# Moving the z, g and half of the output projection of an SSD/retention mixer in among its sample-state updates, and taking q times a retention state before the state is updated, in plain fp32

## The reference, cut to what matters

```python
z, xbc, dt_raw, rq, rk, rv, rg = _split(h @ w_in, AB_SIZES)   # widths 2048, 3072, 32, 1024, 1024, 2048, 2048
...                                                           # causal conv and silu on xbc
y, ssm_h = ssd_scan(xs, dt, a, bm, cm, ssm_h)                 # h = exp(dt a) h + dt x B^T ; y = h C
y = (y + xs * d_skip[:, None]).reshape(...) * jax.nn.silu(z)
y = group_rms(y, SSD_GROUPS) * ssd_norm
r, ret_s = retention_scan(q, k, v, ret_s)                     # S = gamma S + k v^T ; o = q S
r = jax.nn.silu(rg) * group_rms(r.reshape(bsz, l, RET_V), RET_HEADS)
return jnp.concatenate([y, r], axis=-1) @ w_out, conv_buf, ssm_h, ret_s
```

## Time and profile before

| what | us |
|---|---|
| median of 3 runs (2172.78 to 2183.26) | 2179.12 |
| the profiled execution's own time | 2174.99 |
| its span, first to last instruction | 2173.2 |
| TensorE (PE) busy | 1906.6, 88% |
| VectorE (DVE) busy | 1375.7, 63% |
| ScalarE (ACT) busy | 896.0, 41% |
| GpSimd (POOL) busy | 202.1, 9% |
| mean granted TensorE clock | 0.922 |

### The profile page before, as it was taken

How to read it: one execution, slowest core, us unless ns; L and a number is a source line. 1 busy time by engine, 2 the same in 40 slices (tenths; PEclk the granted TensorE clock), 3 DMA queues, 4 the chain that set the end, 5 groups by cost and what they waited for, 6 DMA issues and landing times. The chain is left out here.

```text
span 2173.2 us, 35020 instructions
## 1 busy us (share of the span) xinstructions
PE 1906.6 (88%) x13769; PEld 1744.7 (80%) x13769; DVE 1375.7 (63%) x2352; ACT 896.0 (41%) x1143; POOL 202.1 (9%) x292
## 2 busy tenths in 40 slices
PE   6999886996688768998899999999968698899996
PEld 5999786985355467987779999999956597679996
DVE  4665595698767565448567656665652567557654
ACT  4434344346655445332434334433422532434331
POOL 0001101101111000111110011001001021110011
PEclk9999998899799888998999999999985898999998
DMA  6656852336778424666526656656606266526652
GB/s 179 181 163 188 156 168 65 113 117 189 247 261 298 148 79 114 176 233 232 203 90 182 184 160 191 186 157 195 191 29 163 78 217 229 206 86 174 185 160 82
DMA packets 462782, 361.49 MB, mean 166 GB/s; under 512 B 12297, under 2 KB 435493, under 8 KB 462629
## 3 DMA queue, kind: packets, MB, share of 16 engines
q1 hardware_dynamic: 409056, 254.35, 39.9%
q0 software_dynamic: 20192, 71.95, 10.8%
q10 hardware_dynamic: 33424, 33.70, 4.6%
HBM read 321.49 MB, written 38.66 MB: 166 GB/s over the span
## 5 line engine op out<-in xcount | busy, mean ns | idle before, releaser
L211 DVE TENSOR_TENSOR wlo<-raw,whi 128x2048 fp32r<-128x2048 f32 (+2 forms) x262 | 558.9, 2134 | 268.4 <-ACT whi L205 267.7
L252 PE MATMUL psum<-xnh,whi 128*128 128x264 f32 x2328 | 676.9, 291 | 10.1 <-DVE cols L885 9.8
L253 PE MATMUL psum<-xnl,whi 128*128 128x264 f32 x2328 | 668.7, 287 | 0.0
L254 PE MATMUL psum<-xnh,wlo 128*128 128x264 f32 x2328 | 667.5, 287 | 0.0
L205 ACT ACTIVATE whi<-raw 128x2048 fp32r<-128x2048 f32 (+2 forms) x262 | 463.3, 1770 | 190.7 <-DMA raw<-in_w_ffn_out 76.8
L252 PEld LDWEIGHTS psum<-xnh,whi 128*128 128x128 f32 x2328 | 449.0, 193 | 15.7 <-DVE cols L885 8.6
L253 PEld LDWEIGHTS psum<-xnl,whi 128*128 128x128 f32 x2328 | 448.8, 193 | 1.2
L254 PEld LDWEIGHTS psum<-xnh,wlo 128*128 128x128 f32 x2328 | 445.9, 192 | 0.0
L252 PE MATMUL psum<-Hh,whi 128*128 128x264 f32 x704 | 200.5, 285 | 0.0
L254 PE MATMUL psum<-Hh,wlo 128*128 128x264 f32 x704 | 200.0, 284 | 0.0
L253 PE MATMUL psum<-Hl,whi 128*128 128x264 f32 x704 | 199.1, 283 | 0.0
(11 more groups left out here) (479 smaller groups left out, 3425.3 us busy)
## 6 DMA issues: line engine op xcount, KB each, us to landing
raw<-in_w_ffn_in SPq DMA_DIRECT2D x176, 512.0 KB, 4.9
raw<-in_w_in_ab SPq DMA_DIRECT2D x88, 512.0 KB, 4.4
raw<-in_w_ffn_out SPq DMA_DIRECT2D x64, 384.0 KB, 4.0
raw<-in_w_ffn_out SPq DMA_DIRECT2D x64, 320.0 KB, 3.3
sb<-in_state_ret POOLq DMA_DIRECT2D x32, 512.0 KB, 5.6
out<-sb ACTq DMA_DIRECT2D x32, 512.0 KB, 4.8
raw<-in_w_out_ab SPq DMA_DIRECT2D x32, 512.0 KB, 4.5
kc<-in_cache_mem_k POOLq DMA_DIRECT2D x32, 512.0 KB, 5.9
```

Source lines behind the costliest of these rows:

```text
L211: nc.vector.tensor_tensor(wlo[:, c % SLOTS, 0:m], raw[:, c % SLOTS, 0:m], whi[:, c % SLOTS, 0:m].bitcast(F32), ALU.subtract).then_inc(lo_d ...
L252: e.matmul(out, a, hi[:, kk, 0:S.cols], start=first, stop=False)
L253: e.matmul(out, a, lo[:, kk, 0:S.cols], start=False, stop=False)
L254: m = e.matmul(out, b, hi[:, kk, 0:S.cols], start=False, stop=final)
```

## The change

`Linear` gets a third table, `mid`, whose stages PE runs in the middle of a chunk and DVE and ACT run right behind the split of chunk r+2. Then:

- `SSDSample` is cut in 16 stages of one half state, `RetPrompt` in single scores, values and states; all of them stand in `mid` and `hooks` of the z projection, together with the transposes. `SSDSample` takes one PSUM bank for each half state and spreads B and C rows with one matmul (`spread40`: high parts in rows 0 to 7, remainders in rows 32 to 39 of one tile).
- `RetSample` becomes `RetItem`, one state. PE takes the state as it was loaded as the stationary operand, with one column of q (eight products of 128x128 by 128x1 in fp32), then ACT decays it and DVE adds k v one item later. Since q S_new = gamma (q S_old) + (q.k) v, `RetOut` adds the second term for four tiles of a head. The rounding `sh`, the remainder `sl`, `rrow` and their transposes are gone. States are spread over the g projection and the first half of the output projection, one in each half chunk (four in chunk 0 of g).
- The multiplication by silu(z) and silu(g) for the prompt is put off by one chunk (`gated_late`); the samples' part is kept aside (`zs`, `gs`).
- `Stat` and `Apply` of y and r, group by group, go in the tables of g; the samples' r has its own small `Stat` and `RetSplit`.
- The output projection is two projections of eight chunks: y first (added to x by DVE), then r.
- `mixer_c` uses `Rows40` and `spread40` in place of `SplitRows` and `spread`.

```diff
@@ Linear.pe, in the loop over t and k
+                            if 2 * (t * S.kt + k + 1) == S.tiles * S.kt:
+                                S.hook("pe", e, i, r, S.mid)
@@ Linear.both
                     S.split_later(split, e, i, r + LEAD)
+                    S.hook(which, e, i, r, S.mid)
                     if S.early:
...
+        def spread40(e, out, b, rows):
+            return e.matmul(out, sel[0:40, b:b + 1].to_broadcast([40, P]), rows, start=True, stop=True)
...
+            class SSDSample(Stage):
...
+                def pe(S, e):
+                    u = S.u
+                    if u == 0:
+                        e.wait_ge(rows_lo, bc_rows_ready)
+                    if u >= 2:
+                        e.wait_ge(hy_done, 8 * (u - 1))
+                    c = 256 * (u % 2)
+                    spread40(e, psum[:, 4 + u % 2, :].rearrange("p (q n) -> p q n", q=2), u // 2, BC[:, :, c:c + 256]).then_inc(bcb_done, 1)
...
+            class RetStart(Stage):
+                def pe(S, e):
+                    e.wait_ge(qk_made, 1)
+                    e.wait_ge(hy_done, 16 * NS)
+                    for d in range(2):
+                        m = e.matmul(psum[:, 5, QC:QC + 32], ones[:, :], qks[:, d:8:2, :], start=d == 0, stop=d == 1)
...
+            class RetItem(Stage):
+                def pool(S, e):
+                    j = S.i + SB
+                    if j < N_RET:
+                        e.wait_ge(s_out[buf(j)], 16 * (j // SB))
+                        load_s(e, j)
+                def pe(S, e):
+                    i = S.i
+                    b, h = item(i)
+                    v_row(e, i)
...
+                    e.wait_ge(s_in[buf(i)], 16 * (i // SB + 1))
+                    for t in range(4):
+                        c = OC + (4 * h + t) * NS + b
+                        for d in range(2):
+                            m = e.matmul(psum[:, 5, c:c + 1], sb[:, buf(i), d, t * P:(t + 1) * P], qs[:, 2 * h + d, b:b + 1], start=d == 0, stop=d == 1)
+                    m.then_inc(s_used, 1)
...
+                def act(S, e):
+                    i = S.i
                     if i >= 2:
+                        S.keep(e, i - 2)
+                    e.wait_ge(s_used, i + 1)
+                    v = sb[:, buf(i), :, :]
+                    nc.scalar.activation(v, v, ACT.Copy, scale=gam[item(i)[1]]).then_inc(sdec, 1)
...
+                def dve(S, e):
+                    if S.i >= 1:
+                        S.update(e, S.i - 1)
...
+            def gated_late(dst, stash, q0, final, ready=None):
...
+                def dve(e, l, par, use):
+                    e.tensor_tensor((sg, ht)[par][:, :, :], psum[:, 2 * par:2 * par + 2, 0:T], rstd_two, ALU.mult).then_inc(gate_scaled, 1)
+                    if l >= 1:
+                        mul(e, l - 1, 1 - par)
...
+            points = [[bc_rows, SampleStart()] + v_turn, v_turn2, k_turn,
+                      [RetScores(0, vt_ready)],
+                      [RetValues(0), RetState(0, after_scores(0))],
+                      [RetValues(1), RetScores(1, after_state(0))],
...
+            for u in range(15):
+                points[u + 1].append(SSDSample(u))
+            points[15].extend([SSDSample(15), z_last, SSDOut(), RetStart()])
+            Linear(W, 8, KD, 2, by_cols(W, 0), (xnh, xnl), act=az, dve=dz, mid={c: points[2 * c] for c in range(8)},
+                   hooks={c: points[2 * c + 1] for c in range(8)})
...
+            ret_at = [[RetItem(0), RetItem(1)], [RetItem(2), RetItem(3)]] + [[RetItem(s + 2)] for s in range(2, 30)] + [[], [], []]
...
+            ahead = {0: r_stat(0), 1: y_stat(0)}
+            hook = {0: [], 1: y_apply(0)}
+            ahead[2] = r_stat(1)
+            hook[2] = r_apply(0)
+            ahead[3] = y_stat(1)
+            hook[3] = y_apply(1)
...
+            ahead[4] = r_stat(2) + y_stat(2)
+            hook[4] = r_apply(1)
...
+            Linear(Wo, KD, 16, 1, one_half(0), (yh, yl), ready=y_split, dve=add_y, mid={c: ret_at[16 + 2 * c] for c in range(8)},
+                   hooks={c: hook.get(c, []) + ret_at[17 + 2 * c] for c in range(8)})
+            stages.extend(ret_at[32])
+            r_split = xn_wait()
+            residual(Wo, KD, 16, 1, one_half(1), (rh_, rl_), 1.0, G_X, ready=all_of(r_split, at_least(r_lo, RH)))
@@ mixer_c, SampleC.pe
                         for j in range(2):
-                            m = spread(e, psum[:, S.bank(b) + j, :], b, vsh[:, j * 512:(j + 1) * 512], vsl[:, j * 512:(j + 1) * 512])
+                            m = spread40(e, psum[:, S.bank(b) + j, :], b, vsr[:, j * 512:(j + 1) * 512])
```

More of the change, by code:

```diff
@@ L68, in build @@
         rstd4 = place("rstd4", [P, 4, T], at=tab_at)
+        dtab_at = top[0]
         dtab = place("dtab", [P, RH, NP])
@@ L1583, in mixer_ab @@
-            rr_done = sem_of("ret_rows_turned")
-            yh = place("yh", [P, 16, T], F32R, at=R2)
-            yl = place("yl", [P, 16, T], F32R, at=R2 + 16 * T * 4)
-            y = xbc[:, 0:16, :]
-            az, dz = gated(y, ACT.Silu)
-            Linear(W, 8, KD, 2, by_cols(W, 0), (xnh, xnl), act=az, dve=dz, early=True,
-                   hooks={b: [RetSample(b)] for b in range(NS)})
-            stages.append(RetSampleOut())
-            z_out = evicted()
-            Stat(xbc, 4, 4, rstd4, lambda e, t: (z_out(e), e.wait_ge(rsm_out, 1), [e.wait_ge(q, 64) for q in rS_stored]) if t == 0 else None)
@@ L1595, in mixer_ab @@
-            s_stored = lambda e: [e.wait_ge(q, n) for q, n in zip(s_out, ret_moves)] and None
-            Apply(xbc, 4, 4, rstd4, G_SSD, yh, yl, wait=s_stored)
-            y_split = xn_wait()
-            rh_ = place("rh", [P, 16, T], F32R, at=R1)
-            rl_ = place("rl", [P, 16, T], F32R, at=R0)
-            ag, dg = gated(vf, ACT.Silu)
-            stat, apply, u = {}, {}, tot["use"]
-            for G in range(4):
-                t4 = slice(4 * G, 4 * G + 4)
-                stat[2 * G] = behind(lambda: Stat(vf[:, t4, :], 1, 4, rstd4[:, G:G + 1, :]))
-                apply[2 * G + 1] = behind(lambda: Apply(vf[:, t4, :], 1, 4, rstd4[:, G:G + 1, :], None, rh_[:, t4, :], rl_[:, t4, :],
-                                                        wait=at_least(bank_free, u + 2 * G + 4)))
@@ new lines, in mixer_ab, with y_stat, y_apply @@
+            t4 = lambda G: slice(4 * G, 4 * G + 4)
+            def y_stat(G):
+                first = lambda e, t: (e.wait_ge(ssd_out, 1), e.wait_ge(y_gated, 1), [e.wait_ge(q, 64) for q in rS_stored]) if t == 0 else None
+                return behind(lambda: Stat(xbc[:, t4(G), :], 1, 4, rstd4[:, G:G + 1, :], first if G == 0 else None))
+            def y_apply(G):
+                return behind(lambda: Apply(xbc[:, t4(G), :], 1, 4, rstd4[:, G:G + 1, :], G_SSD + 4 * G, yh[:, t4(G), :], yl[:, t4(G), :]))
@@ new lines, in r_stat, with r_apply, s_stat @@
+            def r_stat(G):
+                return behind(lambda: Stat(vf[:, t4(G), :], 1, 4, rstd_r[:, G:G + 1, :], lambda e, t: e.wait_ge(ro_out, 2 * G + 2) if t == 0 else None, n=NP))
+            def r_apply(G):
+                stored_h = (lambda e: [e.wait_ge(q, 64) for q in hb_out] and None) if G == 0 else None
+                return behind(lambda: Apply(vf[:, t4(G), :], 1, 4, rstd_r[:, G:G + 1, :], None, rh_[:, t4(G), :], rl_[:, t4(G), :], n=NP, wait=stored_h))
+            def s_stat(h):
+                return behind(lambda: Stat(vf[:, t4(h), NP:T], 1, 4, rss[:, h:h + 1, :], lambda e, t: e.wait_ge(rsm_out, h + 1) if t == 0 else None, n=NS))
@@ new lines, in mixer_ab, with one_half, parts @@
+                               (qk_made, 2), (qk_sum, 1), (y_gated, 2)])
+            Wo = A["w_out_ab"][0]
+            def one_half(half):
+                def parts(dst, i, r):
+                    v = dst[:, 0:16 * P].rearrange("p (k n) -> p k n", k=16)
+                    src = Wo[half * 2048:(half + 1) * 2048, :].rearrange("(k p) n -> p k n", p=P)
+                    for a, b in ((0, 8), (8, 16)):
+                        yield v[:, a:b, :], src[:, a:b, bass.ds(i * 512 + r * P, P)]
+                return parts
@@ L2082, in mixer_c @@
             t_ready = turned()
+            v_rows = Rows40(v, vsr, 8, 6, t_ready)
+            v_rows_ready = tot["rows"]
+            stages.append(v_rows)
             class Prompt(Stage):
```

586 lines of the change are left out of this document (288 added, 298 removed).

## The result

The changed kernel takes 2203.0 us (median of 4 runs, 2201.4 to 2206.8), the kernel before 2178.3 beside it. The ratio is 1.0117, with a 95% interval from 1.0089 to 1.0145: slower by 1.2%, where I forecast 2146 us and faster, and outside my range (2098 to 2188). The profiled execution spans 2199.6 us at a mean granted clock of 0.903, against 2173.2 at 0.922.

What follows compares the result with a forecast made beforehand. Parts of a 452 us stretch were bound differently; PE's 181 us of dense work could cover the sample work. 29 us there plus 4.5 in layer 1 made 33 off 2174.99: 2142, or 2146 as median; range 2098 to 2188.

Steps and rivals of the forecast that it cites:

- C: First half of the output projection with 14 states: 5.1 us per half chunk on PE, 82 us in all, ending at 866.
- B: g projection with 18 states and y's and r's statistics: periods of 19 us, one of 24, ending at 779.
- What bounds the kernel now: Stretch of 452 us, parts bound differently, only the output projection PE-full; PE's 181 us of dense work could cover sample work.
- A: z projection under the SSD samples: chunk period 14.6 us, ending at 622, with PE restarting at 624.
- I take 2.0 where PE comes from dense work: Price of one state's 16-record product on PE: 2.0 us behind dense work, 3.0 behind a wait.
- the 5 us put in for r's Apply: Start of the output projection's first half: five us for r's Apply and the product put off.
- D: Second half of the output projection: 8 chunks of 5.65 us, 45 us, ending at 917.
- E: Layer 1: period of 5.50 us loses 1.0 for six of eight samples, transposes cost 1.5; net -4.5 us.
- Rival 2: TensorE's clock stays at 0.50 in the output projection's first half, and g lengthens: 2229 us, slower; chance 0.12.
- Rival 3: Loads at 268 GB/s take 11.7 us a chunk in the output projection's first half, 12 us more: 2158; chance 0.09.
- Rival 4: Chains in the z and g stages are 2.5 us a period longer, +37 us: 2183, no change; chance 0.17.
- Rival 1: Queues interleave better: z period 11.7 us without DVE's waits, g period 16.3 at the upper clock: 2105; chance 0.20.

Runs made afterwards that it cites:

- run 6: Changed kernel with ScalarE doing the hook stages ahead of the chunk's silu in the z projection; ratio 1.0058 to the kernel before.
- run 3: Changed kernel with each state ahead of Apply in the hooks of g's chunks; ratio 1.0049 to the kernel before.
- Run 5: Changed kernel with q standing still and the state moving (4 records for 16), samples' retention output left out; ratio 0.9975 to the kernel before.
- Run 7: Changed kernel with states ahead of Apply, RetOut earlier, product in pieces in y half only: 0.9889 to kernel before; with ScalarE's z order too, 0.9822.
- Runs 1: Changed kernel with the product of q and a state cut in four pieces among the next half chunk's matmuls; ratio 1.0170 to the kernel before.
- run 2: Changed kernel with only the first of each state's four tiles multiplied with q, loads and stores kept; ratio 0.9891 to the kernel before.
- e8_all: Changed kernel with states ahead of Apply, earlier RetOut, pieces in the y half only and ScalarE's hooks before silu in z; 2138.2 us, ratio 0.9822.

## Why the prediction was wrong, point by point

Of the 58 us, 25 were lost in C and 23 in B. The step that failed is the same in both: the dense matmuls behind a state's one-column product were priced at the upper clock (2.83 us for 24), and in C they take 4.6.

**What bounds the kernel now: held.** The stretch, its parts and their bounds were read rightly, and the runs moved the time where these say.

**A, z under the SSD samples: mechanism right, end 8 us late.** The forecast period of 14.6 us with a gap of 2.9 behind each scaling is 14.37 (546.11 to 560.49) with 2.62, and run 6 shows that the gap is ScalarE's order. What failed are the first and the last period. The sum has all the transposes ahead of the first half state and full periods of 14.6 us from there on, but k's transposes and their copies stood behind it:

```profile
511.68 2.16 DVE L1351 SCALAR_TENSOR_TENSOR hb<-psum,xdt,hb 128x128 f32<-128x128 f32 x8 [4.33 <-ACT hb L1325]
...
519.37 0.88 DVE L625 TENSOR_SCALAR k_tm<-psum,tail 128x256 f32<-128x256 f32 x2 [0.75 <-PE psum L604]
523.21 2.16 DVE L1351 SCALAR_TENSOR_TENSOR hb<-psum,xdt,hb 128x128 f32<-128x128 f32 x8 [2.96 <-ACT hb L1325]
```

From the first half state to the third (511.68 to 531.05) it is 19.4 us, 4.8 more than a period. And I gave the last chunk "no `wlo` and evictions behind it" and priced nothing for the samples' V rows, which the diff puts ahead of the last two half states:

```profile
617.16 1.28 DVE L748 TENSOR_TENSOR vsx<-psum,vsx 8x512 fp32r<-8x512 f32 x2 [0.74 <-ACT vsx L742]
619.94 0.68 DVE L748 TENSOR_TENSOR vsx<-psum,vsx 8x512 fp32r<-8x512 f32 x1 [1.50 <-ACT vsx L742]
...
624.05 2.16 DVE L1351 SCALAR_TENSOR_TENSOR hb<-psum,xdt,hb 128x128 f32<-128x128 f32 x8 [1.72 <-ACT hb L1325]
```

From the product of the last scaling (616.4, which is 617.16 less the wait of 0.74) to 624.05 it is 7.6 us, of which the forecast's period already had 2.9 as the wait for the decay; the period of these rows (605.19 to 624.05) is 18.9 us, 4.3 more than forecast. The two make 9 us; the rest of the stage gives 1 back.

**B, g: the chain was right, the clock was not.** From the first matmul of a Stat (669.55) to the end of the update (681.54) the chain takes 12.0 us, forecast 11.2. PE waits 4.4 us in mid chunk (forecast 3.7), ended by the update, and run 3 removes these waits. The period is 20 to 24 us (Stats at 646.22, 669.55, 690.72 and 714.60; 762.97 and 783.34), not 19. Two terms failed. One is "I take 2.0 where PE comes from dense work", with the upper clock for what follows: behind a product at 1.95 us the next half chunk was at the upper clock twice (674.06 to 677.20 and 695.1 to 698.3), but at a clock of 0.62 to 0.65 and 4.3 to 4.6 us long six times (as at 641.7 and 747.3). Run 5, which changes the form of the product alone, gives 12 of the 23 us back. The other is waits that had no term: 6.2 us for RetOut in two and 12.3 for ScalarE's squares in three, 6.9 of them ahead of the small Stat of the samples (726.05), against the 5 us put in for r's Apply. Run 7 shows that those for RetOut can go; those for the squares were not tested by themselves. Chunk 0 erred the other way: three of its four products took 1.95 us and not the lower clock's price, and it came to its end in 14.2 us (632.0 to 646.2), forecast 17, though its first half was mostly at the lower clock.

**C, the y half: this is the step that failed.** "Per half chunk PE has 2.83 + 0.25 + 2.0 = 5.1 us" was right for the product and the spread and wrong for the 24 matmuls, priced at the upper clock. 24 at the lower take 5.3; here they take 4.6 (6.84 less 0.43 and 1.81), some 16 of them at the lower level. 14 half chunks with 1.7 us more are 24 us, the 25 of the table. The 5 us that the sum had for cold stretches went into the first half chunk (5.1 us in place of 2.8) and into RetOut and the samples' Stat, which stretch two half chunks to 7.6 and 9.5. Runs 1, 2, 5 and 7 each bring the clock back in another way and the time with it.

**D: 4 us too short.** The r half begins at the lower clock behind the samples' last statistics, with 27 matmuls in 6.0 us (926.56 to 932.60) in place of 3.2: 3 of the 4. **E: held** (5.1 in the loop, 2 to 4 net).

**The rivals.** Rival 2 is what happened, at chance 0.12. It "decides once C is cold for half of its time", and C's clock of 0.76 is just that; its 2229 assumed 0.50 throughout. Its evidence was in the text: the earlier trace rows has PE full with such products at 0.50. I set against it that half a chunk is dense and that the old stage had 0.90 with its products in between. The second was no counterexample: in those products, L1568 to L1570, 512 columns move, in these one, and run 5 shows the difference. The Trainium skill, "TensorE: Matmul & The Clock Gate", section "Loop structure matters more than you think", has a long wait between matmuls make the clock fall and matmuls back to back keep it up. By that C would have stayed at the upper clock; its rows show the clock fall with no wait at all. Rival 3 was wrong (run 2: with the loads unchanged, C can take 75 us). Rival 4 was right in kind, in the waits for the squares, but the longer chains stood at A's two ends and not in each of its periods. Rival 1 needed orders that the change did not have, and its 11.7 us for a period of A lies below the 12.7 at which PE is full (run 6); e8_all with 0.982, some 2140 us, is about halfway to its 2105.

## What to carry to other kernels

A sum made of durations is only as good as the clock under each. When one-column matmuls move from a stage of their own in between dense ones, try the sum with the dense ones behind them at the lower level as well, and look for the product in the other form (few columns standing still, many moving) or cut it in pieces. When a stage is moved into another's queue, list for each engine what stands ahead of the instruction that others wait for: three edits of order, one of them a single line, and the pieces gave back here what the overlap had promised.

## What the runs showed that I had not expected

- A block of 16 one-column fp32 records (1.8 us, full PE, clock 1.00) is followed, within 0.8 us and with no wait, by some 3.3 us of dense matmuls at 0.50, again and again in step with the half chunks. It is not so behind every block: in g the half chunks at 674.06 and 695.1 came directly behind such a block and ran at 1.00 throughout. What decides between the two, the runs leave open. The same records in fours with six matmuls between them run at 1.00: in e8_all from 765.5 to 792.0, with 26.1 of 26.5 us busy. The whole y half there has 0.92; the rest is mostly its cold start and what follows the two whole products.

```profile
765.50:792.00 26.50, 26.13 (x202) 24.07 (x201) 15.88 (x25) 11.21 (x12) 2.87 (x5) 1.00 0.80 253
```

- The pieces cost next to nothing themselves. The half chunk there is 5.3 to 5.6 us (spreads at 766.34, 771.67 and 777.22), against 5.1 by the sum of its parts.
- In fp32, 128x128 by 128x1 eight times (16 records) and 128x8 by 128x512 twice (4 records) take the same time, 1.95 and 1.88 us. The Trainium skill, "TensorE: Matmul & The Clock Gate", section "LDWEIGHTS (loading the stationary operand)", has a load of 128 columns take 107 ns; 16 of them would be 1.7 us, an estimate by the page. From the first record to the next matmul it is 1.81 us (841.43 to 843.24), 0.113 a record, and the measured number stands; at the lower clock the same 16 take 3.57.
